# Load order of the second chunk's weights, GpSimd's order of sums, and the squares of the last norm, in a two-layer encoder on one core

## What is computed

```python
def _rms(x, g):
    xf = x.astype(jnp.float32)
    y = xf * lax.rsqrt(jnp.mean(xf * xf, axis=-1, keepdims=True) + EPS)
    return (y * g.astype(jnp.float32)).astype(x.dtype)
...
    h = _rms(x, ffn_norm[l])
    x = x + (jax.nn.silu(h @ w_gate[l]) * (h @ w_up[l])) @ w_down[l]
...
    return _rms(x, final_norm)
```

## Time and profile before

| what | us |
|---|---|
| median of 3 runs | 2282.66 (2282.36 to 2284.16) |
| the profiled execution | 2283.84 |
| its span in the profile | 2282.0 |

### The profile page before, as it was taken

One profiled execution on the slowest core, in us unless ns is written; L12 is line 12 of the kernel. 1 busy time (PEld: TensorE's weight loads), 2 busy tenths in 40 slices (PEclk: granted clock), 3 DMA queues, 4 the chain that ended last, 5 costly groups with the idle time before them and its releaser, 6 DMA issues.

```text
span 2282.0 us, 31255 instructions
## 1 busy us (share of the span) xinstructions
PE 2238.9 (98%) x10600; PEld 1862.5 (82%) x10600; DVE 1805.9 (79%) x2794; ACT 984.0 (43%) x1876; POOL 993.2 (44%) x689
## 2 busy tenths in 40 slices
PE   8999999999999999999999999999999999999997
PEld 6888888888888888788888888888888888887886
DVE  6998388888787877989958873987966666679997
ACT  4556134544444444443324541455444444443442
POOL 4314100125777777788600010001255455577883
PEclk9999999999999999999999999999999999999998
DMA  8533542233666666843243136323323232376421
GB/s 305 219 110 135 198 168 91 93 130 127 223 221 234 221 234 232 330 138 103 92 148 111 56 130 221 111 74 111 120 79 111 97 110 97 110 261 241 139 72 77
DMA packets 93463, 346.89 MB, mean 152 GB/s; under 512 B 9760, under 2 KB 9888, under 8 KB 74016
## 3 DMA queue, kind: packets, MB, share of 16 engines
q1 hardware_dynamic: 92624, 344.53, 43.1%
q10 hardware_dynamic: 720, 0.86, 0.1%
HBM read 237.35 MB, written 108.00 MB: 151 GB/s over the span
## 4 chain that ended last, share of the span: by engine, by line
PE 85%; DVE 6%; issue 2%; POOL 1%; ACT 1%; DMA 0%; DVEq 0%; SPq 0%; ACTq 0%; POOLq 0%
PE bank L520 27%; PE bank L522 27%; PE bank L521 27%; PE bank L1162 2%; PE bank L1000 1%; PE bank L1008 1%; DVE x L2212 1%; DVE aT_lo L2031 1%; PE bank L526 1%; PE bank L527 1%; DVE u L2178 1%; DVE qpe L1906 1%; DMA raw<-in_wffn 0%; POOL slot L913 0%; DVE y_out L2314 0%
## 5 line engine op out<-in xcount | busy, mean ns | idle before, releaser
L898 POOL TENSOR_TENSOR slot<-raw,slot 128x512 fp32r<-128x512 f32 x160 | 223.3, 1399 | 234.4 <-ACT slot L1610 234.4
L520 PE MATMUL bank<-h_hi,slot 128*128 128x512 f32 x640 | 249.0, 389 | 0.0
L521 PE MATMUL bank<-h_lo,slot 128*128 128x512 f32 x640 | 249.0, 389 | 0.0
L522 PE MATMUL bank<-h_hi,slot 128*128 128x512 f32 x640 | 249.0, 389 | 0.0
L875 POOL TENSOR_TENSOR acc<-sq,zero 128x512 f32<-128x512 f32 x6 | 6.7, 1116 | 546.1 <-ACT sq L1399 546.1
L520 PE MATMUL bank<-u,slot 128*128 128x512 f32 x560 | 220.2, 393 | 7.8 <-POOL slot L913 7.0
L521 PE MATMUL bank<-u,slot 128*128 128x512 f32 x560 | 219.7, 392 | 0.0
L522 PE MATMUL bank<-u,slot 128*128 128x512 f32 x560 | 219.6, 392 | 0.0
L520 PE MATMUL bank<-h_hi,w 128*128 128x512 f32 x512 | 203.4, 397 | 0.0
L898 POOL TENSOR_TENSOR slot<-s_stage,slot 128x512 fp32r<-128x512 f32 x120 | 175.9, 1466 | 60.2 <-ACT slot L1610 58.7
L2212 DVE TENSOR_TENSOR x<-x,bank 128x512 f32<-128x512 f32 x280 | 177.5, 678 | 28.3 <-PE bank L522 28.3
(11 more groups left out here) (255 smaller groups left out, 5931.5 us busy)
## 6 DMA issues: line engine op xcount, KB each, us to landing
w<-parked SPq DMA_DIRECT2D x81, 1024.0 KB, 4.8
raw<-in_wffn SPq DMA_DIRECT2D x112, 512.0 KB, 3.4
u_kept<-made SPq DMA_DIRECT2D x148, 256.0 KB, 2.9
uf<-u_kept SPq DMA_DIRECT2D x70, 512.0 KB, 5.6
parked<-w SPq DMA_DIRECT2D x27, 1024.0 KB, 6.3
parked<-p SPq DMA_DIRECT2D x27, 1024.0 KB, 4.9
raw<-in_watt SPq DMA_DIRECT2D x27, 512.0 KB, 5.0
praw<-in_watt SPq DMA_DIRECT2D x27, 512.0 KB, 5.8
```

The lines of the kernel that those rows point to most:

```text
L520: nc.tensor.matmul(out_ap, lhs[0], rhs[0], start=first, stop=False, skip_group_check=joins)
L521: nc.tensor.matmul(out_ap, lhs[0], rhs[1], start=False, stop=False, skip_group_check=joins)
L522: return nc.tensor.matmul(out_ap, lhs[1], rhs[0], start=False, stop=last, skip_group_check=joins)
L898: nc.gpsimd.tensor_tensor(slot[i][:, 1, :], gate_source(i), slot[i][:, 0, :].bitcast(F32), ALU.subtract).then_inc(s_gate_lo.sem, 1)
```

## The change

- SyncE: in step d=0 the loads of the first raw chunk for d=1 (`next_raw(G7, 0)`) are issued before the load of u G4 that waits for the residual sums.
- GpSimd: in every step the order is low part of G1, a_sum for both q, low parts of G5 and G2, the differences into G7's place for both q, G6's, N3's, and the low parts of G4, N3, G6, G7. The counts on which ScalarE waits follow it. The number of operations is the same, 22 in a step.
- VectorE, both layers: the additions of plain products 0 to 3 stand between the undone sums, one behind each pair.
- Last norm: ScalarE writes the squares of request 0 into eight tiles of their own (in slots whose weights are used up); GpSimd adds squares 0 to 3, VectorE 4 to 7 (`second_add`), and TensorE takes both sums (`first_sums`, eight small products in place of four) before plain product 10 (SUMS_BEFORE 2 in place of 6). The spread of request 0's root stands before product 13 instead of behind product 15. For request 1 GpSimd adds squares 0 to 3, and TensorE adds squares 4 to 7 one by one into the same bank; VectorE adds none and joins no partial sums. The order of VectorE's additions, roots and outputs is written anew.

```diff
@@ -209,7 +209,8 @@
...
 POOL_SQUARES = 4
-SUMS_BEFORE = 6
+SUMS_BEFORE = 2
+SPREAD_BEFORE = 5
@@ -394,6 +395,9 @@
...
         acc_out = at("acc_out", [P, T], r_yv + 16 * KB)
+        sq_first = at("sq_first", [P, KT, T], r_w)
+        acc_first = at("acc_first", [P, T], r_w + 16 * KB)
+        acc_second = at("acc_second", [P, T], r_w + 18 * KB)
@@ -484,6 +488,9 @@
...
         s_final_acc = sem("final_squares_added")
+        s_sq_first = sem("first_request_squares")
+        s_acc_first = sem("first_request_low_squares_added")
+        s_acc_second = sem("first_request_high_squares_added")
@@ -787,10 +794,10 @@
...
                 next_u(G2)
+                next_raw(G7, 0)
...
                     load_u(l, 1, G4)
-                next_raw(G7, 0)
@@ -913,26 +920,27 @@
...
-            def down_sums(l, d):
-                for q in range(2):
-                    a11, a21, a22 = down_source(q, G1), down_source(q, G7), down_source(q, G4)
-                    pool.wait_ge(s_down_raw[q][0], raw_value(l, d, q))
+            def down_weights(l, d):
...
+                sources = [(down_source(q, G1), down_source(q, G7), down_source(q, G4)) for q in range(2)]
...
+                def made(n, q):
+                    return s_a_sum.layer_at(l, 8 * d + 2 * n + q)
...
+                down_lo(l, d, G1)
+                for q, (a11, a21, a22) in enumerate(sources):
...
                     nc.gpsimd.tensor_tensor(a_sum[q][:], a21, a22, ALU.add).then_inc(s_a_sum.sem, 1)
+                down_lo(l, d, G5)
+                down_lo(l, d, G2)
+                for q, (a11, a21, a22) in enumerate(sources):
                     nc.gpsimd.tensor_tensor(a21, a11, a21, ALU.subtract).then_inc(s_a_sum.sem, 1)
...
-            def down_weights(l, d):
...
-                down_lo(l, d, G1)
-                down_sums(l, d)
                 for q in range(2):
-                    pool.wait_ge(s_a_sum.sem, s_a_sum.layer_at(l, 8 * d + 2 * q))
+                    pool.wait_ge(s_a_sum.sem, made(0, q))
...
                         s_a_sum.sem, 1)
-                down_lo(l, d, G5)
-                down_lo(l, d, G2)
                 for q in range(2):
-                    pool.wait_ge(s_a_sum.sem, s_a_sum.layer_at(l, 8 * d + 4 + q))
+                    pool.wait_ge(s_a_sum.sem, made(2, q))
@@ -975,8 +983,15 @@
...
                     last.then_inc(s_a_lo.sem, 1)
-                add_squares("next", l)
...
+                if l < L - 1:
+                    add_squares("next", l)
...
+            pool.wait_ge(s_sq_first, 2)
+            nc.gpsimd.tensor_tensor(acc_first[:], sq_first[:, 0, :], sq_first[:, 1, :], ALU.add).then_inc(s_acc_first, 1)
+            for k in range(2, POOL_SQUARES):
+                pool.wait_ge(s_sq_first, k + 1)
+                pool.wait_ge(s_acc_first, k - 1)
+                nc.gpsimd.tensor_tensor(acc_first[:], acc_first[:], sq_first[:, k, :], ALU.add).then_inc(s_acc_first, 1)
@@ -1289,9 +1304,13 @@
...
-            def final_sums(squares):
+            def first_sums():
...
+                pe.wait_ge(s_acc_first, POOL_SQUARES - 1)
+                pe.wait_ge(s_acc_second, KT - POOL_SQUARES - 1)
                 for m in range(NT):
-                    last = nc.tensor.matmul(bank[0][:, m:m + 1], squares[:, m * P:(m + 1) * P], ones[:, 0:1], start=True,
+                    nc.tensor.matmul(bank[0][:, m:m + 1], acc_first[:, m * P:(m + 1) * P], ones[:, 0:1], start=True, stop=False)
+                    last = nc.tensor.matmul(bank[0][:, m:m + 1], acc_second[:, m * P:(m + 1) * P], ones[:, 0:1], start=False,
@@ -1299,12 +1318,10 @@
...
                         if l == L - 1 and b == 1 and n == SUMS_BEFORE:
-                            f, sq0, add0, st0, t0, x0 = norm_counts("next", l)
-                            pe.wait_ge(s_add.sem, f(s_add, add0 + KT - 1))
-                            final_sums(acc)
+                            first_sums()
+                        if l == L - 1 and b == 1 and n == SPREAD_BEFORE:
+                            spread((s_final, ROOT_LINKS), s_pe, rstd, 2)
                         plain_down(l, b, n)
-                if l == L - 1:
-                    spread((s_final, ROOT_LINKS), s_pe, rstd, 2)
@@ -1349,19 +1366,20 @@
...
-            def last_sums(squares, at):
+            def last_sums(squares):
                 for m in range(NT):
-                    last = nc.tensor.matmul(bank[at][:, m:m + 1], squares[:, m * P:(m + 1) * P], ones[:, 0:1], start=True,
-                                            stop=True)
-                last.then_inc(s_pe, 1)
...
-            pe.wait_ge(s_act, 7)
-            last_sums(sq_out[:, 6, :], 0)
-            pe.wait_ge(s_final_acc, 5)
-            last_sums(acc_out, 5)
-            pe.wait_ge(s_act, 8)
-            last_sums(sq_out[:, 7, :], 3)
-            spread((s_final, 2 * ROOT_LINKS + 2), s_pe, yy, 1)
+                    last = nc.tensor.matmul(bank[3][:, m:m + 1], squares[:, m * P:(m + 1) * P], ones[:, 0:1], start=False,
+                                            stop=True, skip_group_check=True)
+                return last
...
+            nc.tensor.matmul(bank[3][:, 0:NT], ident[:], zero[:].to_broadcast([P, NT]), start=True, stop=True)
+            pe.wait_ge(s_final_acc, POOL_SQUARES - 1)
+            last_sums(acc_out)
+            for k in range(POOL_SQUARES, KT):
+                pe.wait_ge(s_act, k + 1)
+                last = last_sums(sq_out[:, k, :])
+            last.then_inc(s_pe, 1)
+            spread((s_final, 2 * ROOT_LINKS), s_pe, yy, 1)
@@ -1623,7 +1641,7 @@
...
                     else:
-                        n = {G5: 2 * q, N3: 6 + q, G6: 4 + q, G7: 2 * q + 1}[g]
+                        n = {G5: q, N3: 6 + q, G6: 4 + q, G7: 2 + q}[g]
@@ -1766,14 +1784,17 @@
...
                     last.then_inc(s_a_hi.sem, 1)
-                for k in range(KT):
-                    norm_square("next", l, 0, k)
-                    if l < L - 1:
+                if l < L - 1:
+                    for k in range(KT):
+                        norm_square("next", l, 0, k)
...
+            act.wait_ge(s_prod.sem, s_prod.layer_at(L - 1, NPROD * ND - 1))
+            for k in range(KT):
+                act.wait_ge(s_xf.sem, s_xf.layer_at(L - 1, k))
+                nc.scalar.activation(sq_first[:, k, :], x[:, 0, k, :], ACT.Square).then_inc(s_sq_first, 1)
...
                 act.wait_ge(s_xf.sem, s_xf.layer_at(L - 1, KT + k))
-                act.wait_ge(s_prod.sem, s_prod.layer_at(L - 1, NPROD * ND - 1))
@@ -2287,8 +2308,9 @@
...
                     sums_undone(m)
+                    down_add(m)
                 dve.wait_ge(s_back.sem, s_back.layer_at(l, 2 * MH - 1))
-                for ev in range(KT):
+                for ev in range(MH, KT):
@@ -2304,40 +2326,45 @@
...
-            def final_add(k):
-                dve.wait_ge(s_act, k + 1)
-                dve.wait_ge(s_final_acc, k - 1)
-                nc.vector.tensor_tensor(acc_out[:], acc_out[:], sq_out[:, k, :], ALU.add).then_inc(s_final_acc, 1)
+            def second_add(k):
+                dve.wait_ge(s_sq_first, k + 1)
+                if k == POOL_SQUARES + 1:
+                    nc.vector.tensor_tensor(acc_second[:], sq_first[:, k - 1, :], sq_first[:, k, :], ALU.add).then_inc(
+                        s_acc_second, 1)
+                else:
+                    dve.wait_ge(s_acc_second, k - POOL_SQUARES - 1)
+                    nc.vector.tensor_tensor(acc_second[:], acc_second[:], sq_first[:, k, :], ALU.add).then_inc(s_acc_second, 1)
...
-            for k in range(6):
-                down_add(KT + k)
+            second_add(5)
+            second_add(6)
+            down_add(KT)
+            second_add(7)
+            down_add(KT + 1)
...
             assert n[0] == ROOT_LINKS, n
-            down_add(KT + 6)
-            down_add(KT + 7)
+            for k in range(2, 5):
+                down_add(KT + k)
...
             output(0, 0)
+            down_add(KT + 5)
             output(0, 1)
+            down_add(KT + 6)
             output(0, 2)
-            final_add(4)
-            final_add(5)
-            for m in range(3, KT):
+            down_add(KT + 7)
+            for m in range(3, 6):
                 output(0, m)
-            mean = ms[2][:]
-            dve.wait_ge(s_pe, 3)
-            final(nc.vector.tensor_scalar(mean, bank[0][:, 0:NT], 1.0 / D, EPS, ALU.mult, ALU.add))
+            rsqrt_column(final, D, bank[3][:, 0:NT], (s_pe, 3), s_final)
+            n[0] += 1
+            assert n[0] == 2 * ROOT_LINKS, n
+            output(0, 6)
+            output(0, 7)
             dve.wait_ge(s_pe, 4)
-            final(nc.vector.scalar_tensor_tensor(mean, bank[5][:, 0:NT], 1.0 / D, mean, ALU.mult, ALU.add))
-            rsqrt_column(final, D, bank[3][:, 0:NT], (s_pe, 5), s_final, eps=mean)
-            n[0] += 1
-            assert n[0] == 2 * ROOT_LINKS + 2, n
-            dve.wait_ge(s_pe, 6)
...
```

## The result

| | before | after | ratio |
|---|---|---|---|
| median, us | 2284.2 (2282.22 to 2285.94, 21 runs) | 2287.67 (2285.39 to 2290.95, 21 runs) | 1.0016 (1.0009 to 1.0023) |
| profiled span, us | 2282.0 | 2284.5 | |

What follows compares the result with a forecast made beforehand. TensorE, busy 98% of the span, was taken as the bound, with VectorE beside it without slack in d=0. Terms 4.9 + 0 + 0.5 - 2.6 = +2.8 us on the median 2282.66 gave 2285.5 us, range 2267.5 to 2294.0.

Steps and rivals of the forecast that it cites:

- Loads and start of GpSimd: Down stage, d=1: weight loads issued at about 941 and 942 us, GpSimd starting at 949.2, 4.3 us earlier.
- VectorE later from d=0's new order: Down stage, d=0: GpSimd's order, and with it VectorE, runs later by 0 to 2.3 us, 0.9 taken.
- Blocked operations: VectorE's four made sums and u pair beside a busy GpSimd lose 4.1 to 6.3 us, 5.3 taken.
- Clock: TensorE's slow restart after the wait before G7 of d=0 costs 2.4 us for each layer.
- The down stage: The wait at G7 replaces the stall at G5: +2.0 us in layer 0, +2.9 in layer 1, +4.9 together.
- G4: GpSimd's G4 split in later steps: cover of 0.5 us, cost taken as zero, up to 1.5 us each.
- rival (c): G4 late in every later step: +12.0 us at most, +8 taken, 2293.5 us; chance 0.10.
- (a): Both stalls at G5 simply vanish, -12.1, with the end -14.7 us, 2268.0 us; chance 0.20.
- (b): GpSimd meets only two of VectorE's six operations, 2.2 us; -7.6 us in all, 2275.1 us; chance 0.12.
- The seam between the layers: Layer 0, product 8: GpSimd's square sums beside the undone sums cost 0 to 1.7 us, 0.5 taken.
- The end: Behind the last product and before it, the new squares bring request 1's outputs sooner by 2.0 to 4.3 us, 2.6 taken.
- four sums 0.7: Kernel's end: four sums behind the last product take 0.7 us of the 5.7 us before request 1's outputs.

Runs made afterwards that it cites:

- e2: Only GpSimd's new order, put into the kernel before; 2276.51 us, ratio 0.9971.
- e1: Only the new load order, put into the kernel before; 2288.04 us against 2282.98.
- e9: Kernel before with early loads, GpSimd's new order from d=1 on, and GpSimd held behind G1's first split until VectorE's u split of G7; 2274.55 us, ratio 0.9955.
- e10: e9 without GpSimd's added wait in d=1; 2291.03 us in a single run.
- e5: Changed kernel with GpSimd held at the start of d=1 until VectorE has made its u split of G7; 2279.28 us against 2283.41, ratio 0.9978.
- e3: Squares alone: changed kernel with the load order and GpSimd's order of before; 2285.16 us, ratio 1.0004.
- e7: e3 with VectorE adding squares 4 and 5 of request 1, so 16 small products behind the last large one instead of 20; 2282.26 us against 2283.41, ratio 0.9995.
- e8: Kernel before with three useless GpSimd additions behind VectorE's additions of G4 in d=0; 2282.37 us in a single run, beside 2283.41.
- e4: Changed kernel with VectorE's four made sums moved behind N3's additions; 2278.71 us, ratio 0.9979.
- e6: Changed kernel with VectorE's four made sums moved behind G7's additions of d=0; 2279.24 us, ratio 0.9983.
- e12: The changed kernel run a second time; 2286.96 us, ratio 1.0015 against the kernel before.
- e11: e9 with the change's squares and VectorE adding the pair of squares as in e7; 2276.07 us, ratio 0.9962.

## Why the prediction was right, point by point

**Loads and start of GpSimd: right.** Forecast, plus the 0.47 us of offset: loads at 941.5 and 942.5, GpSimd at 949.7. Measured 941.80, 943.52 and 949.89, with TensorE as the releaser, as said.

**VectorE later from d=0's new order: right.** Taken 0.9 (0 to 2.3). G4's additions start at 948.78 - 0.47 = 948.31 for 947.36: 0.95. e2, with the order alone, shows its price as the 0.52 us wait at G6; kernels with the old order in d=0 (e1, e9, e10) don't have it.

**Blocked operations: right in kind, size at the lower end.** Taken 5.3 us of 4.1 to 6.3; measured 1.94 + 2.14 = 4.1. I chose the upper half because GpSimd has no gap. It had none, but VectorE's first two made sums passed at 0.68 us, and it was GpSimd's split that was held (951.15, 2.45 us). With that, G7 comes at 959.94 instead of 960.6 + 0.47. The 6.3 is real as well: where GpSimd is at work a little ahead of the first made sum, all six are blocked, 9.85 - 3.87 = 6.0 us in e1. The Trainium skill, page "SBUF — State Buffer", section "SBUF: two separate sides", has the shared port as an exclusive lock that goes to whoever starts first, for a whole instruction. The blocked 1.66 to 1.78 us agree, and so does the fall back to 0.68 as soon as GpSimd is held in e5. The 2.45 us split fits the lock, but not simply the one who starts first: its record begins at 951.15, 0.02 us ahead of the first made sum (951.17), and yet it is the split that took 1.15 us more than its 1.30 us, while two sums in a row passed at 0.68.

**Clock: right as a mean.** Taken 2.4 us per layer. Excess less the gaps (0.68 at G6 and 5.03 - 0.23 = 4.80 at G7, and the same within 0.01 in layer 1) leaves 1.67 in layer 0 and 2.70 in layer 1, mean 2.2.

**The down stage: the direction right, the size too high.** +2.0 and +2.9 forecast, 0.0 and +1.9 measured: 1.2 per layer from the wait itself (6.7 late forecast, 0.68 + 4.80 = 5.5 measured); the clock took 0.7 less in layer 0 and 0.3 more in layer 1. In layer 0 an old stall with its dear clock (3.1 us) is replaced by a longer one with a cheap clock. That is luck of the two executions: in e3 and e7, behind the same old stall, the clock took only 1.8 to 1.9, and against them the changed down stage costs 3.5 and 2.7 us, nearer to the forecast.

**G4 (term 0, rival (c) up to +12): right.** No wait for GpSimd's split anywhere in the changed kernel. It is real but small: 1.1 to 1.4 us, only in d=1, and only where GpSimd starts late (e2, e5). Later steps have none. Rivals (a) and (b) fell with the wait; e9 shows what (a) would have been worth, -10.3 where I had -14.7, since it doesn't bring the gain at the end and keeps 1.23 us per layer.

**The seam between the layers: right within its ends.** +0.5 taken, 0 measured (923.40 us in both). GpSimd's sums did meet one undone sum, 1.71 us long in the changed kernel, and the cover of 1.6 us took it.

**The end: wrong.** -2.6 taken (-4.3 to -2.0), +0.2 measured. Up to the last product all held: small products at 0.22 us, a wait for VectorE's sums of 1.43 (0.6 to 2.2), the last start 3.1 us later (2.3 to 3.9). The step that failed is the term "four sums 0.7" behind the last product, with its own addition and square ahead of it. TensorE takes its work in order, and the sums of acc_out and of all four single tiles were queued behind the last product: 20 small products, 2267.10 to 2272.81, of which only the last four need the last square. That is 5.7 us for the forecast 2.1; 0.9 of it is the clock, which fell during the last sixteen (4.68 us, and 3.75 in e3), and the rest is their number. The root took 1.8 and the spread 1.1, as said. So 8.7 us from the last product to request 1's outputs instead of 5.7, and 0.5 us gained instead of 2.6. The outputs' own end gave back 0.7 more (3.3 for 2.6 us from the last output to the end). The change moves a 512 KB store of request 0 to right in front of request 1's stores, and these then take 2.8 us to land (median of eight) instead of 2.1; that it is the cause was not tried.

Two errors, 3.0 us too much in the down stage and 2.8 too little at the end, nearly cancel. The total is closer than its terms deserve, and that is luck.

## What to carry to other kernels

Before an engine is let loose earlier, look at who works beside it at its new time. Here the stall was removed by moving two-input work of GpSimd beside two-input work of VectorE, and it came back at VectorE's next consumer, at up to 1.7 us for each 0.6. The early start wasn't needed: GpSimd's new order alone gave -6.6 us, and an added wait that keeps GpSimd away turned +3.6 us into -5, and with the old order in d=0 (and the old squares) into -10. In a tail, count what stands in each engine's queue behind the last large operation, not only what depends on it.

## What the hardware showed that I had not expected

**The clock after a wait has no fixed price.** Excess less gaps: 3.1 and 1.9 us behind the 3.5 and 3.8 us gaps of before, 1.8 behind 3.6 in e3, 2.15 behind 3.8 in e8 (there TensorE ran seven starts at full clock first, and slowed only from 959.23), 1.7 and 2.7 behind 4.8, 2.2 to 2.7 behind 6.5 in e1 and e10. Behind gaps of 2.4 and less (e2, e4, e5, e6, e9) it is 0.3 or less. In e7 it is 1.9 behind 3.75 and 4.04. So over these waits of 3.5 to 6.5 us the loss hardly follows the length: it lies between 1.7 and 3.1, and the dearest is behind the shortest of them. What sets it wasn't tried.

**A short wait with small products behind it can cost the clock as well.** In kernels with the new squares the sums of request 0 start 15.56 us behind the last u product, each time after a wait of about 1.4 us. The spread comes 21.5 us behind it in the changed kernel, e12 and e11, but 23.1 in e3, e4, e5, e6 and e7. Windows of the changed kernel and of e4, 17.5 to 19.5 us behind that product (columns as above):

```profile
2258.53:2260.53 2.00, 2.00 (x10) 1.63 (x10) 1.72 (x10) 0.00 (x0) 0.53 (x1) 1.00 0.00 0
```

```profile
2246.09:2248.09 2.00, 2.00 (x6) 1.61 (x6) 1.61 (x9) 0.00 (x0) 0.52 (x1) 0.50 0.00 0
```

The same tail, the same wait and the same eight products, and in one the granted clock is 1.00, in the other 0.50, for 1.6 us of loss. e7 and e11 have the same code there too and differ. What decides isn't known; no run was made on it. As each is a single profiled execution, it isn't shown either that the difference goes with the kernel and not with the execution.

The clock fell among the last 16 small products as well: in the changed kernel from 1.00 to 0.50, and they took 4.68 us (4.64 in e12), while the same 16 took 3.75 in e3 and 3.87 in e5. So in these runs the changed kernel and e12 lose 0.9 at the very end, e3 and e5 lose 1.6 before it, and e4 and e6, with 4.93 and 4.98 us, lose at both. That is a part of why e4 and e6 fell short. Without its 1.6 us the end of e3 would be 42.5, 0.8 shorter than before.
